# Attention scores as two 64-row tiles, shared normalised operands, halved first units and a re-planned order in a single-core transformer block

## What is computed

```python
# layer A: differential attention (6 pairs of heads, 64 deep), memory attention (4 heads), squared-ReLU MLP
h = _rmsnorm(x, a_norm_attn); z = h @ a_w_in; q, k = rope(q), rope(k)
s = einsum('bqhcd,bkhcd->bhcqk', q, k) * 64 ** -0.5        # causal mask, softmax
o = rmsnorm(einsum('bhqk,bkhe->bqhe', p[:, :, 0] - lam * p[:, :, 1], v), subln)
kv = _rmsnorm(mem, mem_norm) @ w_mem_kv                    # memory keys and values, for A and for B
x = x + concat(o_self, o_mem) @ w_out
x = x + square(relu(_rmsnorm(x, norm_mlp) @ w_up)) @ w_down            # 1024 -> 4096 -> 1024
# layer B: 12 causal heads; its keys come from another norm of the same x
kv = _rmsnorm(x, kv_norm) @ w_kv;  z = _rmsnorm(x, b_norm_attn) @ b_w_in
# last layer: indexed attention (top 64 keys of each query, 8 heads), retention with decays (8 heads), gated MLP
r = (q_b k_b^T * decay, lower triangle) @ v_b
x = x + concat(o_a, group_norm(r) * silu(gate)) @ w_out_2
x = x + (silu(h @ w_gate_2) * (h @ w_up_2)) @ w_down_2
```

## Time and profile before

| | |
|---|---|
| median of three runs | 949.27 us |
| the profiled execution: its time, its span | 949.11 us, 947.4 us |
| TensorE busy (share of the span), matmul records | 929.2 us (98%), 6326 |
| VectorE, ScalarE, GpSimd busy | 580.2 us, 476.1 us, 54.5 us |
| bytes moved by DMA | 157.87 MB, mean 167 GB/s |
| share of TensorE in the chain that ended last | 95% |

### The profile page before, as it was taken

One profiled execution on the slowest core, in us unless ns is written; L12 is line 12 of the kernel. 1 busy time (PEld: TensorE's weight loads), 2 busy tenths in 40 slices (PEclk: granted clock), 3 DMA queues, 4 the chain that ended last, 5 costly groups with the idle time before them and its releaser, 6 DMA issues.

```text
span 947.4 us, 16451 instructions
## 1 busy us (share of the span) xinstructions
PE 929.2 (98%) x6326; PEld 784.3 (83%) x6326; DVE 580.2 (61%) x785; ACT 476.1 (50%) x701; POOL 54.5 (6%) x120
## 2 busy tenths in 40 slices
PE   6999999999999999999999999999998999999998
PEld 5788888888888888888888888888877888888887
DVE  4777767566665666636865555578886564454444
ACT  5766565444444366572744444566336464443441
POOL 3001121000000010001100000011100000000000
PEclk9999999999999999999999999999999999999999
DMA  8934225655555543404755555474521265655541
GB/s 287 313 112 165 100 77 185 219 178 182 202 201 203 172 149 133 144 36 156 249 197 177 195 198 183 141 226 174 178 67 45 61 208 187 205 184 177 188 166 45
DMA packets 95441, 157.87 MB, mean 167 GB/s; under 512 B 5928, under 2 KB 37624, under 8 KB 95392
## 3 DMA queue, kind: packets, MB, share of 16 engines
q1 hardware_dynamic: 93872, 155.09, 48.3%
q10 hardware_dynamic: 1488, 2.10, 0.8%
q0 software_dynamic: 32, 0.02, 0.0%
HBM read 156.12 MB, written 1.06 MB: 166 GB/s over the span
## 4 chain that ended last, share of the span: by engine, by line
PE 95%; DVE 3%; issue 1%; ACT 1%; DMA 0%; SPq 0%; DVEq 0%; ACTq 0%
PE proj L1494 10%; PE proj L1496 10%; PE proj L1495 10%; PE proj L1550 8%; PE turn L1550 8%; PE score L1550 8%; PE outp L1550 8%; PE score L1709 3%; PE score L1494 3%; PE score L1496 3%; PE outp L1496 3%; PE outp L1494 3%; PE score L1495 3%; PE outp L1495 3%; PE turn L1521 2%; PE outp L1754 2%
## 5 line engine op out<-in xcount | busy, mean ns | idle before, releaser
L1833 DVE TENSOR_TENSOR wlo<-raw,whi 128x2048 fp32r<-128x2048 f32 x145 | 328.0, 2276 | 216.1 <-ACT whi L1282 150.2
L1282 ACT ACTIVATE whi<-raw 128x2048 fp32r<-128x2048 f32 x64 | 121.7, 1913 | 171.6 <-PE score L1550 85.2
L1276 ACT ACTIVATE whi<-raw 128x2048 fp32r<-128x2048 f32 (+1 forms) x81 | 153.0, 1903 | 70.5 <-PE score L1550 32.2
L1494 PE MATMUL proj<-whi,set 128*128 128x512 f32 (+1 forms) x432 | 172.0, 398 | 1.4 <-DVE wlo L1833 1.4
L1496 PE MATMUL proj<-whi,set 128*128 128x512 f32 (+1 forms) x432 | 167.7, 388 | 0.0
L1495 PE MATMUL proj<-wlo,set 128*128 128x512 f32 (+1 forms) x432 | 167.3, 387 | 0.0
L1550 PE MATMUL score<-whi,set 64*128 64x512 f32 x448 | 139.9, 387 | 0.0
L1550 PE MATMUL outp<-whi,set 64*128 64x512 f32 x448 | 139.8, 387 | 0.0
L1494 PEld LDWEIGHTS proj<-whi,set 128*128 128x128 f32 x432 | 81.6, 189 | 17.7 <-issue 2.1
L1496 PEld LDWEIGHTS proj<-whi,set 128*128 128x128 f32 x432 | 81.5, 189 | 17.1
L1495 PEld LDWEIGHTS proj<-wlo,set 128*128 128x128 f32 x432 | 81.7, 189 | 15.2
(11 more groups left out here) (224 smaller groups left out, 1422.0 us busy)
## 6 DMA issues: line engine op xcount, KB each, us to landing
raw<-in_a_w_up SPq DMA_DIRECT2D x32, 512.0 KB, 4.4
raw<-in_a_w_down SPq DMA_DIRECT2D x32, 512.0 KB, 4.4
raw<-in_b_w_up SPq DMA_DIRECT2D x32, 512.0 KB, 4.4
raw<-in_b_w_down SPq DMA_DIRECT2D x32, 512.0 KB, 4.3
raw<-in_w_gate SPq DMA_DIRECT2D x22, 512.0 KB, 3.9
raw<-in_w_up SPq DMA_DIRECT2D x22, 512.0 KB, 4.9
raw<-in_w_down SPq DMA_DIRECT2D x22, 512.0 KB, 4.0
raw<-in_a_w_in SPq DMA_DIRECT2D x20, 512.0 KB, 6.2
```

Source lines behind the costliest of these rows:

```text
L1276: act.activation(shaped(whi, u), shaped(raw, u), ACT.Copy).then_inc(hi_done, 1)
L1282: act.activation(shaped(whi, u), shaped(raw, u), ACT.Copy).then_inc(hi_done, 1)
L1494: pe.matmul(out_, hi, wh, start=start, stop=False)
L1833: dve.tensor_tensor(shaped(wlo, u), shaped(raw, u), shaped(whi, u), ALU.subtract).then_inc(lo_done, 1)
```

## The change

- **Scores.** `headq` and its zeroing are gone. A step `scores` now serves two items; head 0 is multiplied on rows 0 to 63 and written to score bank 0, head 1 on rows 64 to 127 and to bank 1. The causal masks of both items are one bf16 matmul of 384 columns for each bank. Both banks come free when the second item's exponentials are done. The steps `exps` hold what VectorE and ScalarE do for each item. The four retention score steps are tiled in the same way.
- **Shared operands.** For the memory and for layer B the gain moves into the weights: 14 units are split with a gain per row (`hi_blocks`, `lo_blocks`, four instructions of 512 columns in place of one of 2048). The memory is turned once and x once less.
- **Start.** The first two units are loaded, split and multiplied in halves with a semaphore for each half. ScalarE's queue loads the first gains. TensorE transposes the identity 14 and 24 times ahead of the work (`warm_up`); ScalarE runs one copy early.
- **Decays** are applied by ScalarE while it copies from PSUM, and GpSimd zeroes the triangle in place (`affine_select`), with two result buffers in turn.
- **MLPs.** `in_row_tiles`, `up_tiles` and `down_tiles` are gone; all matmuls of the MLPs use 128 rows (`up_pair`, `half_unit`), with waits for each unit and bank.
- **Order.** MOVES is new for all three engines.

```diff
@@ MOVES @@
-        ("multiply 78", "turn_operand 42"), ("attend 37", "attend 38"), ("multiply 77", "turn_weights 39"),
...
+        ("multiply 74", "turn_operand 34"), ("turn_weights 38", "attend 37"), ("attend 35", "attend 36"),
...
+HALVED = 2
+WARM = (14, 24)
...
-    def chunk_units(w, cols):
-
-        return [unit(w, h * UK * P, cols) for h in range(2)]
+    def chunk_units(w, cols, gain=None):
+
+        return [unit(w, h * UK * P, cols, gain=None if gain is None else GAINS.index(gain) * KT + UK * h)
...
-        cmask = sb("cmask", [P, P], BF16)
+        cmask = sb("cmask", [P, 3, P], BF16)
...
-        def pairs(a, first, n):
-
-            return [(ALL, slice(a, a + n), lambda t: qk[:, first:first + n, tok(t)], 1.0)]
-
-        def heads(a, first, n, scale=1.0):
-
-            return [(LOW, slice(a, a + n), lambda t: headq[LOW, first:first + n, 0, tok(t)], scale),
-                    (HIGH, slice(a, a + n), lambda t: headq[HIGH, first:first + n, 1, tok(t)], scale)]
+        def pairs(a, first, n, scale=1.0):
+
+            return [(ALL, slice(a, a + n), lambda t: qk[:, first:first + n, tok(t)], scale)]
...
+        def both_s(release):
+
+            n = count.s
+            count.s += 2
+            f = [free["S", b] for b in range(2)]
+            free["S", 0] = free["S", 1] = release
             return n, f
...
-            it.s, it.s_free = s_use((exp_done, it.exp + 1))
             ITEMS.append(it)
-            st = add("scores")
-            st.it = it
+            if len(ITEMS) % 2 == 0:
+                first = ITEMS[-2]
+                first.at, it.at = 0, first.n
+                st = add("scores")
+                st.items = [first, it]
+                st.s, st.s_free = both_s((exp_done, it.exp + 1))
+                for i in range(2):
+                    ex = add("exps")
+                    ex.it, ex.s, ex.last = st.items[i], st.s, it.i
...
-            return turn_operand(mem_nat, h, [(g_at(name), 1, UK * h)], (mem_landed[h], 16), free)[-1]
+        def turn_mem(h):
...
-        turn_kv = lambda h: turn_operand(x, h, [(g_at("kv_norm"), 0, UK * h)], (resid_done, r1.r + 2), 2 * last + 2)[-1]
-        xk = [half_around(lambda: turn_kv(h), q0, h, 1, xb[h], "O") for h in range(2)]
+        for h in range(2):
+            mul_chunk_half(q0, h, 0, xb, "O")
...
+            load_half(0, 0)
+            load_half(0, 1)
+            load_memory(1)
+            load_half(1, 0)
+            load_half(1, 1)
+            u = HALVED
...
+                if st.kind == "retention_scores":
+                    for a in range(2):
+                        n = TOK - a * P
+                        pool.wait_ge(decayed, 2 * st.p + a + 1)
+                        block = ret[st.p % 2][a].rearrange("p (c n) -> p c n", c=2)[:, :, 0:P]
+                        pool.affine_select(out=block, in_=block, compare_op=ALU.is_ge, fill=0.0, base=0,
...
+                if u < HALVED:
+                    for i, done in enumerate((hi_half, hi_done)):
+                        act.wait_ge(half_landed[u][i], 16)
+                        hi_blocks(u, range(2 * i, 2 * i + 2)).then_inc(done, 1)
+                    return
...
+            def hi_blocks(u, ks):
+
+                g = UNITS[u].gain
+                if g is None:
+                    ks = slice(ks[0], ks[-1] + 1)
+                    return act.activation(shaped(whi, u)[:, ks, :], shaped(raw, u)[:, ks, :], ACT.Copy)
+                act.wait_ge(gain_cols, 1 if g < FIRST * KT else 3)
+                for k in ks:
+                    ins = act.activation(shaped(whi, u)[:, k, :], shaped(raw, u)[:, k, :], ACT.Copy,
+                                         scale=gcol[:, g + k:g + k + 1])
+                return ins
...
+            load_gains(act, 0)
+            act.wait_ge(consts_made, 1)
+            act.activation(junk1[:], ident[:], ACT.Copy).then_inc(act_warm, 1)
+            act.wait_ge(act_warm, 1)
...
+                elif st.kind == "retention_scores":
+                    act.wait_ge(s_full, st.s + 2)
+                    for a in range(2):
+                        n = TOK - a * P
+                        if st.p > 1:
+                            act.wait_ge(o_full, ret_out[st.p - 2] + 1)
+                        elif st.p == 0:
+                            act.wait_ge(rope_done, 2 * rq.rope + 2)
+                        else:
+                            act.wait_ge(bias_stored, 16)
+                        for c in range(2):
+                            h = 2 * st.p + c
+                            ins = act.activation(ret[st.p % 2][a][:, c * n:(c + 1) * n], Sb[c][:, a * TOK:a * TOK + n],
+                                                 ACT.Copy, scale=dec[:, a, 8 + h:9 + h])
+                        ins.then_inc(decayed, 1)
...
+            def first_half(lhs, bank):
+
+                wh, wl = shaped(whi, 0), shaped(wlo, 0)
+                pe.wait_ge(hi_half, 1)
+                for t in range(NT):
+                    for k in range(2):
+                        pe.matmul(bank[t][:], set_hi[lhs][:, k, tok(t)], wh[:, k, :], start=k == 0, stop=False)
+                        pe.matmul(bank[t][:], set_lo[lhs][:, k, tok(t)], wh[:, k, :], start=False, stop=False)
+                pe.wait_ge(lo_half, 1)
+                for t in range(NT):
+                    for k in range(2):
+                        pe.matmul(bank[t][:], set_hi[lhs][:, k, tok(t)], wl[:, k, :], start=False, stop=False)
...
+            def warm_up(n):
+
+                for _ in range(n):
+                    pe.transpose(Ob[1][:, 0:P], ident[:], ident[:])
...
-                    up_tiles(u, h, st.hset, step + 2 * h, multiplied)
+                    for q, pair in enumerate((Pp, Tp)):
+                        if h == 0 and first and q == 0:
+                            for t in range(NT):
+                                wait(st.freed[t])
+                        elif h == 0 and not first:
+                            pe.wait_ge(up_added, j * 2 + (st.up0 + q + 1))
...
-                down_tiles(u0 + 2, st.uset, first, multiplied + 4)
+                for c, b in enumerate("SO"):
+                    u = u0 + 2 + c
+                    pe.wait_ge(lo_done, at(u + 1, 4))
+                    if first:
+                        pe.wait_ge(up_added, st.up0 + 2 - c)
+                    for t in range(NT):
...
-                    S = Sb[it.s % 2]
-                    for c in range(2):
-                        o = c * it.n
-                        ins = pe.matmul(S[:, o:o + it.n], headq[:, it.q, c, tok(it.t)], it.k[:, 0:it.n],
...
+                    if kind in ("diff", "causal"):
+                        for c in range(2):
+                            add_mask(c, Sb[c][:, 0:3 * P], identb[:], cmask[:, :, :].rearrange("p b n -> p (b n)"))
+                    for it in st.items:
+                        for c in range(2):
+                            S = Sb[c][:, it.at:it.at + it.n]
+                            if kind == "idx":
+
+                                c0 = P - P * it.t
+                                add_mask(c, S, flip[:], btoep[it.pair // 2][:, 2 * it.pair % 4 + c, c0:c0 + it.n])
+                                add_mask(c, S, identb[:], selmask[:, it.t, 0:it.n])
+                    for i, it in enumerate(st.items):
+                        for c in range(2):
+                            ins = pe.matmul(Sb[c][:, it.at:it.at + it.n], qk[HALF[c], it.q, tok(it.t)],
+                                            it.k[HALF[c], 0:it.n], start=not opened[c], stop=i == 1)
+                            opened[c] = True
+                            if i == 1:
+                                ins.then_inc(s_full, 1)
                 elif st.kind == "turn_weights":
...
+                        wait(st.s_free[c])
+                    for a in range(2):
                         for c in range(2):
-                            ins = pe.matmul(Sb[s % 2][:, c * n:(c + 1) * n], headq[:, 4 + st.p, c, tok(a)],
-                                            qk[:, Q_QB + st.p, a * P:TOK], start=True, stop=True)
-                        ins.then_inc(s_full, 1)
+                            ins = pe.matmul(Sb[c][:, a * TOK:a * P + TOK], qk[HALF[c], 4 + st.p, tok(a)],
+                                            qk[HALF[c], Q_QB + st.p, a * P:TOK], start=a == 0, stop=a == 1)
+                            if a == 1:
+                                ins.then_inc(s_full, 1)
...
                     it = st.it
-                    dve.wait_ge(s_full, it.s + 1)
-                    S = Sb[it.s % 2][:, 0:2 * it.n].rearrange("p (c n) -> p c n", c=2)
-                    dve.tensor_reduce(it.nm, S, AX_X, ALU.max, negate=True).then_inc(nmax_done, 1)
+                    dve.wait_ge(s_full, st.s + 2)
+                    dve.tensor_reduce(it.nm, Sp[:, :, it.at:it.at + it.n], AX_X, ALU.max, negate=True).then_inc(nmax_done, 1)
```

307 lines of the change are left out of this document (131 added, 176 removed), and 106 rows, old and new, of the table MOVES.

## The result

The changed kernel takes **927.96 us**, median of 4 runs (926.39 to 928.42), against 949.2 (948.95 to 949.72) before: ratio 0.9773, 95% interval 0.9756 to 0.979. It is faster, as forecast, but by 21.2 us and not by 14, and the time lies just under the range given (928 to 945). The profiled execution took 928.42 us with a span of 926.7, 20.7 less than before.

A forecast was written before the change was run, and what follows sets the result against it. The prediction took TensorE, busy 929.2 of 947.4 us, to bound the kernel. Its terms, -5.2 - 3.5 - 1.5 - 2.5 - 1.2 = -13.9, took 949.1 to 935.2 us, range 928 to 945.

The forecast's parts named there:

- 1. start: Kernel start: halved first units and identity transposes in idle time bring unit 2's first product from 27.29 to 22.1, -5.2 us.
- 2. transposes: Shared operands: 32 transposes fewer on TensorE at 0.109 us each, splits in four pieces costing nothing, -3.5 us.
- 3. MLPs: Two MLPs: 14 chunks at 22.07 instead of 22.12 us and two runs of tiles fewer, together -1.5 us.
- 4. scores: Score steps: eight passes take 5 places instead of 8, with 0.40 us per step for changing to tiles and back, -2.5 us.
- 5. waits: Indexed attention and retention: 36 products cover the first indexed scores' wait, -2.5; added waits +0.5 and +0.8; sum -1.2 us.
- Unit 2's own limit of 22.1: Start: unit 2's DMA landing at 17.92, its copy and low part allow its first product not before 22.1 us.
- full overlap: Rival on scores: passes of the two tiles pair up wholly, -7.5 instead of -2.5 us, total 930.2; chance 0.17.
- shared banks: Rival on scores: both score banks held until the second item's exponentials end stop TensorE in 24 steps, 956.8 us; chance 0.06.
- +0.5 for the close retention steps: Part of the waits term: last three retention steps stand close and wait for ScalarE's copies and GpSimd, +0.5 us.
- +0.8 for the shared banks: Part of the waits term: score steps wait for both banks, free about 3.8 us after a step's start, +0.8 us.
- start stays bound: Rival on the start: still bound by loads and splits, -1.5 instead of -5.2 us, total 938.9; chance 0.13.
- no overlap: Rival on scores: plain fp32 passes of the two tiles do not overlap, +8.9 instead of -2.5 us, total 946.6; chance 0.12.

The follow-up runs named there:

- e13: The changed kernel unaltered, run again beside e14 on one chip, five runs: 928.03 us.
- e15: Changed kernel with 32 transposes done twice, as many as the change took away: 931.51 us.
- e4: Kernel before, with only the MLPs' middle chunks on 128 rows as in the changed kernel: 947.44 us beside 949.51.
- e2: Changed kernel with every score pass on all 128 rows instead of one 64-row tile: 935.45 us.
- e1: Changed kernel without the 24 warm-up transposes behind the first memory block, the 14 ahead kept: 928.7 us.
- e6: Changed kernel with 20 warm-up transposes early and 12 behind the first memory block, instead of 14 and 24: 926.16 us.
- e7: Changed kernel with 20 and 12 warm-up transposes as in e6, and the gains turned behind the first memory block instead of ahead: 925.78 us.
- e14: The kernel of e7 unaltered, run again beside the changed kernel on one chip, five runs: 925.65 us.
- e3: Changed kernel with score passes issued head by head (both items of head 0, then both of head 1) instead of alternating: 927.27 us.
- e5: Changed kernel with the score passes of both heads on the upper 64 rows, one tile only: 942.81 us.
- e10: Changed kernel with one entry of TensorE's order undone, first indexed scores behind the gate's 36 products again: 936.87 us.
- e9: Changed kernel with the retention's decays back on VectorE, moved in its order to where their scores are there: 932.27 us.

## Why the prediction was wrong, and where it was right

What I had said, what the runs showed, in us:

| step | forecast | measured | by |
|---|---|---|---|
| 1. start | -5.2 | -1.5 (one group of runs), -3.5 (the other) | unit 2's first product, e13 |
| 2. transposes | -3.5 | -3.3 | e15, rest |
| 3. MLPs | -1.5 | -1.9 | e4, two MLPs |
| 4. scores | -2.5 | -8.1 for the tiles, about -9.6 with the new layout of the steps | e2, rest; starts added up, below |
| 5. waits | -1.2 | -2.7, and -0.9 of clock | below |

1. **Start, wrong.** The step that failed is "the 38 transposes of the identity fill TensorE's idle time and end before the data is there". The last 24 start when the memory block is turned, at 8.39, and end at 12.1; where fewer are in the way, the first product starts at 9.71 (e1) or 9.85 (e6). From "near 8" to 12.11 the parts are these. Some 2.0 us are the half pace of the transposes, since at the full pace the same 24 end at 10.1 (e13). About 0.2 are the transposes themselves (10.08 against 9.85 in e6). 1.0 are the gains: I put the first product behind the data alone and took the gains to be out of the way once they had left SyncE's queue, but they land at 6.4, 1 us later than before, and hold the turned block back (9.85 in e6, 8.85 in e7). The last 0.85 are my estimate of the loads and halves, which was too short (8.85 in e7, 9.51 in e14, so these parts are good to some 0.7). Unit 2's own limit of 22.1 was not reached by any kernel (22.98 in e7); what bounds there is left open.
2. **Operands, right** in size. That the splits in four pieces cost nothing agrees with TensorE's waits, none of which is for a unit's parts behind the start.
3. **MLPs, right**, a little small.
4. **Scores, wrong, and most of the miss.** The step is "TensorE starts what it is given in order; then only head 0's second pass lies beside head 1's first". No row supported it; it was a model. e3 shows that passes of the two tiles are not bound to each other's order, and e5 that the gain is the other tile's. The rival full overlap had the right mechanism, and I gave it 0.17. Its -7.5 is a price for the whole step, masks included, so it compares with about -9.6; charged with the measured 0.30 in place of 0.40 it would have been -9.9. With the rival as I had priced it, the forecast would have been 930.2. The rule that the Trainium skill (TensorEngine Tiling (Array Packing), Overview, Theoretical Speedup) gives, up to twice the speed for 64 rows or less, is what the passes show: 0.65 us of the step (0.85 less 0.20), against 1.31 in e2. The Trainium skill's rule on the change of mode (TensorEngine Tiling (Array Packing), Tiling Modes, Key Properties) holds too: it returns with each step, but at 0.30 us and not at the 0.40 that I had read from the earlier trace rows.
5. **Waits, right in sign, too small.** TensorE's idle time behind unit 2's first product fell from 9.28 us (920.11 less 910.83 busy) to 6.54 (900.88 less 894.34). I had half of it eaten by waits of the shared banks; none of TensorE's waits over 0.3 us is for a score bank, so that rival (0.06) is out. The +0.5 for the close retention steps is there (waits of 0.20 and 0.27 us), the +0.8 for the shared banks is not. The stretch at a granted clock of 0.95 in the earlier trace rows is at 1.00 now; e4 shows 0.9 us for that, but e4 had the waits of the earlier trace rows too, so it isn't shown that this 0.9 comes from the change. What I had not seen is how much hangs on this part: without the one entry of the order it loses 8.9 us (e10), with the decays on VectorE 4.2 (e9). Neither is a gain over the kernel before, which had an order of its own that suited it; they are what the changed kernel loses without them.

Measured terms with the start at -1.5 make -18.4 of the 20.7 us. The other 2.3 us can be placed by adding up the distances between TensorE's starts behind unit 2's first product, waits left out, by kind of row. Scores and masks take 47.3 us in e4 (the attention of the kernel before, at a granted clock of 1.00), 45.8 in e2 and 36.4 in the changed kernel, where the rows behind the tiles give 1.4 of the difference from e2 back. So 1.5 us go with the merged masks and the steps of two items, and the products outside the MLPs take 0.65 less. No run changes either alone. Tiles writing one bank from both heads, as the old layout would have had them, weren't tried.

The rival "start stays bound" came true in its number (-1.5) for another reason than the one given: not loads and splits, but work put ahead of the product. The rivals "no overlap" and "shared banks" did not occur. The two large misses, -5.6 on the tiles and +3.7 on the start, have opposite signs, and that is luck: with the start as forecast the kernel would have taken about 924, and the total would have been off by 11 us and not by 7.

## What to carry to other kernels

Pair up contractions of 64 rows in two row tiles with a bank each wherever they come in twos: they then took half the time, in both orders of issue tried, and each time that the program goes into tiles and out costs 0.30 us. Put TensorE's warm-up where it would be idle anyway, and end it before the first operand is there: here 20 transposes early and 12 late gave 1.8 us in the median over 14 and 24, as all four runs then lay in the lower group. When an edit changes how long a step holds an engine, write the order anew and price a wait with the clock that it costs behind it: 4.9 us more of idle time here cost 8.9.

## What was not expected of the hardware

- Passes of a plain fp32 matmul on one row tile run ahead of earlier issued ones on the other (e3: 1.28 us a step in either order).
- Going into row tiles costs 0.09 us and out of them 0.20 (346.30 and 347.37 above; e5 has the same 0.20, with one tile in use). A 64-row pass alone takes as long as one on all rows (e5, 1.31 us for eight).
- TensorE's granted clock was 0.50, with products 0.42 to 0.43 apart, behind 2.11 idle us at the start (e1) and behind a wait of 4.53 in the middle of the program (e10; one of 1.79 had ended 3.2 us before it began), and 0.51 behind one of 2.78 (e9). Behind the wait of 1.82 in the earlier trace rows it fell in the kernel before and stayed in e4; behind 1.6 idle us at the start the pace went either way (e13 and the first profile of the same kernel), behind 0.36 to 0.80 it stayed (e6, e7).
- The granted clock's column read 1.00 while the products of the earlier trace rows were 0.43 apart, and 1.00 while transposes took 0.22 us each (1.97 for 8 in the changed kernel, 1.09 in e13): the pace of the rows tells more than the column.
